# A low-rank gate product with its operands turned: activations stationary, 32 weight columns moving, sums in side banks and transposed back

## The reference, cut to what matters

```
h = rms_norm(x, norm_g)                  # (tokens, 2048)
proj = h @ w_in                          # c_lr: 16 of its columns
...
log_a = jax.nn.log_sigmoid((c_lr @ w_gate_lr + b_gate).astype(jnp.float32)) / C_GATE_TAU
o_c, new_S = gla_chunked(gq, gk, gv, log_a.reshape(bsz, L, C_HEADS, C_DK), gla_state)
```

## Time and profile before

| what | value |
|---|---|
| median of 3 runs | 2250.97 us (2250.37 to 2251.05) |
| profiled execution | 2249.99 us, its span 2248.2 us |
| TensorE busy (products, loads) | 2242.2 us, 2221.8 us |
| VectorE, ScalarE, GpSimd busy | 1378.3 us, 986.1 us, 77.6 us |
| share of the 16 DMA engines, mean rate | q1 42.7%, q0 5.3%; 162 GB/s |
| granted clock over the run | 1.00 |

### The profile page before, as it was taken

The page is one execution under the profiler, slowest core; times in us unless marked ns, Lnnn a source line. Parts: engine busy times, 40 slices in busy tenths (PEclk is TensorE's granted clock), DMA queues, the critical chain, the costliest instruction groups (busy, mean ns, idle before and its releaser), DMA issues.

```text
span 2248.2 us, 40404 instructions
## 1 busy us (share of the span) xinstructions
PE 2242.2 (100%) x16658; PEld 2221.8 (99%) x16658; DVE 1378.3 (61%) x2457; ACT 986.1 (44%) x1786; POOL 77.6 (3%) x122
## 2 busy tenths in 40 slices
PE   9999999999999999999999999999999999999999
PEld 9999999999999999999999999999999999999999
DVE  7777868765545555546657777777655545545443
ACT  6454356544333333333344543556443333333332
POOL 1100100000000000000011001000000000000000
DMA  8443754334444444445564447543344444444454
GB/s 301 147 160 125 242 197 148 114 131 150 149 149 150 149 149 150 149 150 196 191 227 134 160 134 243 196 141 113 132 150 150 150 150 150 151 150 150 151 198 149
DMA packets 100071, 364.12 MB, mean 162 GB/s; under 512 B 12288, under 2 KB 13056, under 8 KB 99056
## 3 DMA queue, kind: packets, MB, share of 16 engines
q1 hardware_dynamic: 89472, 318.91, 42.7%
q0 software_dynamic: 10128, 42.43, 5.3%
q10 hardware_dynamic: 288, 0.21, 0.0%
HBM read 341.65 MB, written 20.50 MB: 161 GB/s over the span
## 4 chain that ended last, share of the span: by engine, by line
PE 99%; DVE 1%; ACT 0%; issue 0%; ACTq 0%; DVEq 0%
PE main L1715 92%; PE side L1715 5%; PE side L1719 1%; PE side L1935 0%; ACT probs L1420 0%; PE side L1858 0%; DVE ta L536 0%; DVE w_lo L517 0%; DVE probs L947 0%; PE side L1942 0%; DVE probs L951 0%; PE side L1866 0%; DVE probs L912 0%; ACT w_hi L1229 0%; DVE probs L914 0%
## 5 line engine op out<-in xcount | busy, mean ns | idle before, releaser
L517 DVE TENSOR_TENSOR w_lo<-raw,w_hi 128x512 fp32r<-128x512 f32 x1184 | 785.3, 697 | 498.3 <-ACT w_hi L1229 492.9
L1715 PE MATMUL main<-xg_hi,w_hi 128*128 128x320 f32 x3488 | 1083.7, 311 | 2.2 <-DVE w_lo L517 2.2
L1715 PE MATMUL main<-xg_lo,w_hi 128*128 128x320 f32 x3488 | 1077.2, 309 | 0.0
L1715 PE MATMUL main<-xg_hi,w_lo 128*128 128x320 f32 x3456 | 1067.9, 309 | 0.0
L1229 ACT ACTIVATE w_hi<-raw 128x512 fp32r<-128x512 f32 x1184 | 709.6, 626 | 698.2 <-PE main L1715 667.8
L1715 PEld LDWEIGHTS main<-xg_hi,w_hi 128*128 128x128 f32 x3488 | 654.8, 188 | 6.0 <-DVE w_lo L517 2.7
L1715 PEld LDWEIGHTS main<-xg_lo,w_hi 128*128 128x128 f32 x3488 | 654.9, 188 | 0.0
L1715 PEld LDWEIGHTS main<-xg_hi,w_lo 128*128 128x128 f32 x3456 | 648.7, 188 | 0.0
L1715 PE MATMUL main<-branch_hi,w_hi 128*128 128x320 f32 x768 | 237.3, 309 | 0.0
L1715 PE MATMUL main<-branch_lo,w_hi 128*128 128x320 f32 x768 | 237.3, 309 | 0.0
L1715 PE MATMUL main<-branch_hi,w_lo 128*128 128x320 f32 x768 | 237.3, 309 | 0.0
(11 more groups left out here) (259 smaller groups left out, 1292.6 us busy)
## 6 DMA issues: line engine op xcount, KB each, us to landing
raw<-in_w_stream SPq DMA_DIRECT2D x595, 512.0 KB, 3.3
state<-in_state POOLq DMA_DIRECT2D x16, 512.0 KB, 4.7
out_state_s<-state POOLq DMA_DIRECT2D x16, 512.0 KB, 3.9
turned<-normed SPq DMA_DIRECT2D x40, 80.0 KB, 2.1
x_first<-in_x_pairs SPq DMA_DIRECT2D x7, 320.0 KB, 7.4
w_pool<-in_w_pool POOLq DMA_DIRECT2D x2, 1024.0 KB, 6.5
cache_k<-in_cache_k POOLq DMA_DIRECT2D x2, 1024.0 KB, 5.1
cache_v<-in_cache_v POOLq DMA_DIRECT2D x2, 1024.0 KB, 8.2
```

What stands on the lines that cost most here:

```text
L517: dve.tensor_tensor(w_lo[Q % RAWS][:, half], raw[Q % RAWS][:, half], w_hi[Q % HIS][:, half].bitcast(F32), ALU.subtract).then_inc(lo_ready, 1)
L1715: return pe.matmul(out, lhsT, rhs, start=start, stop=stop)
```

## The change

The operands of the rank products are turned. Each of the 16 k tiles of `xg_hi` and `xg_lo` is the stationary operand in three pieces of tokens (`TOKEN_TILES`: 128, 128 and 64), and the tile's 32 useful weight columns (16 high, 16 low) are moved. The sums, tokens on the partitions and 32 columns wide, gather in side banks 1, 2 and 3 in place of a bank of `main`. The four copies of the 16 columns are no longer made by the splits. Instead VectorE copies the finished sums out of PSUM four times side by side (`rank_tok`, which lies in the memory of `tc`), and `rank_turn`, after the block of beat 10, transposes the three pieces into side bank 0. VectorE scales that into `ta`. The gate step moves from beat 10 to 11, `log_decay_sum` from 12 to 13 and `decay_scan` from 13 to 14. The main group of the rank products is gone, so groups are numbered without it.

```diff
-    put(10, "gate", 0, (0, 1, 2, 3))
+    put(11, "gate", 0, (0, 1, 2, 3))
...
-            t = w_hi[Q % HIS][:, half].rearrange("p (k h c) -> p k h c", k=4, h=GH)
-            return t[:, :, :, at:at + RANK]
+            t = w_hi[Q % HIS][:, half].rearrange("p (k c) -> p k c", k=4)
+            return t[:, :, at:at + RANK]
...
-                    dve.tensor_tensor(ta[:, 0, :], group_psum(GROUPS * l + LR_GROUP)[:, 0, :], rstd[:, :],
-                                      ALU.mult).then_inc(main_free, 1)
-                    marks[("lr", l, 0)] = (main_free, GROUPS * l + LR_GROUP + 1)
-                if beat == 12:
+                    four = lambda t: t.unsqueeze(2).to_broadcast([t.shape[0], t.shape[1], 4, 2 * RANK])
+                    v(dve.tensor_copy(rank_tok[:, 0:2, :].rearrange("p i (q c) -> p i q c", q=4),
+                                      four(side[:, 1:3, 0:2 * RANK])))
+                    v(dve.tensor_copy(rank_tok[0:SMP, 2:3, :].rearrange("p i (q c) -> p i q c", q=4),
+                                      four(side[0:SMP, 3:4, 0:2 * RANK])))
+                    v.mark("rank_tok", l, 0)
+                if beat == LR_AT + 2:
+                    dve.wait_ge(rank_turned, l + 1)
+                    dve.tensor_tensor(ta[:, 0, :], rank_psum, rstd[:, :], ALU.mult).then_inc(rank_taken, 1)
+                    marks[("lr", l, 0)] = (rank_taken, l + 1)
+                if beat == 13:
                     log_decay_sum(l)
-                if beat == 13:
+                if beat == 14:
                     decay_scan(l)
...
-                out = main[:, 2 * (G % 2), 0:TOK]
                 for s in range(2):
                     pe.wait_ge(lo_ready, Q * 2 + (s + 1))
                     for kk in range(4):
-                        k, c = k0 + 4 * s + kk, 512 * s + P * kk
-                        both = w_hi[Q % HIS][:, c:c + P]
-                        mm(out, both, xg_hi[:, k, :], first and s == 0 and kk == 0, False)
-                        ins_ = mm(out, both, xg_lo[:, k, :], False, last and s == 1 and kk == 3)
+                        c = 512 * s + P * kk
+                        for x in (xg_hi, xg_lo):
+                            for i, (lo, hi) in enumerate(TOKEN_TILES):
+                                ins_ = mm(side[0:hi - lo, 1 + i, 0:2 * RANK], x[:, k0 + 4 * s + kk, lo:hi],
+                                          w_hi[Q % HIS][:, c:c + 2 * RANK], first and s == 0 and kk == 0 and x is xg_hi,
+                                          last and s == 1 and kk == 3 and x is xg_lo)
                     ins_.then_inc(half_used, 1)
+
+            def rank_turn(l):
+
+                if l == 0:
+                    pe.wait_ge(consts_in, 64)
+                wait_mark(pe, "rank_tok", l, 0)
+                wait_mark(pe, "rms_taken", l, 0)
+                for i, (lo, hi) in enumerate(TOKEN_TILES):
+                    last = turn(rank_psum[:, lo:hi], rank_tok[0:hi - lo, i, :])
+                last.then_inc(rank_turned, 1)
```

More of the change, by code:

```diff
@@ L57 @@
 BEATS = IN_BEATS + MIX_BEATS + OUT_BEATS
-GROUPS = 1 + N_IN + PAIRS * 6 + PAIRS
+GROUPS = N_IN + PAIRS * 6 + PAIRS
 BR_A, BR_B, BR_C = 0, 1, 2
@@ L68, in first_beat @@
     return 4 * g if g < LR_AT // 4 else LR_BEATS + 4 * g
-def group_no(g):
-    return g if g < LR_AT // 4 else g + 1
-LR_GROUP = LR_AT // 4
+TOKEN_TILES = ((0, P), (P, SEQ), (SEQ, TOK))
 C_COS, C_SIN, C_IDENT, C_BLOCK, C_KEEP, C_INVC, C_BSEL, C_END = 0, 320, 640, 768, 896, 1216, 1280, 1288
@@ L291, in trunk @@
         tb = place("tb", [P, 2, TOK])
+        rank_tok = place("rank_tok", [P, 3, P], at=top[0])
         tc = place("tc", [P, 2, TOK])
@@ L360, in trunk @@
         rms_psum = side[:, 0, 0:TOK]
+        rank_psum = side[:, 0, 0:TOK]
         raw_in = [sem(f"raw_in{i}") for i in range(RAWS)]
@@ L384, in trunk @@
         rms_done = sem("rms_done")
+        rank_turned = sem("rank_turned")
+        rank_taken = sem("rank_taken")
         x_hi_ready = sem("x_hi_ready")
@@ L474, in rank_columns @@
         def rank_columns(Q, half, at):
-            t = w_hi[Q % HIS][:, half].rearrange("p (k h c) -> p k h c", k=4, h=GH)
-            return t[:, :, :, at:at + RANK]
+            t = w_hi[Q % HIS][:, half].rearrange("p (k c) -> p k c", k=4)
+            return t[:, :, at:at + RANK]
         def rank_source(Q, half):
-            t = raw[Q % RAWS][:, half].rearrange("p (k c) -> p k c", k=4)[:, :, 0:RANK]
-            return t.unsqueeze(2).to_broadcast([P, 4, GH, RANK])
+            return raw[Q % RAWS][:, half].rearrange("p (k c) -> p k c", k=4)[:, :, 0:RANK]
         block = ctx.enter_context(nc.Block())
@@ L572, in take @@
             def take(l, g):
-                G = GROUPS * l + group_no(g)
+                G = GROUPS * l + g
                 end = last_half(l, first_beat(g) + 3)
@@ L1096, in mix_pair @@
                 Q0 = BEATS * l + IN_BEATS + 18 * j
-                G0 = GROUPS * l + 1 + N_IN + 6 * j
+                G0 = GROUPS * l + N_IN + 6 * j
                 for n in range(3):
@@ L1122, in out_pair @@
                 Q0 = BEATS * l + IN_BEATS + MIX_BEATS + 4 * j
-                G = GROUPS * l + 1 + N_IN + 6 * PAIRS + j
+                G = GROUPS * l + N_IN + 6 * PAIRS + j
                 for part in range(4):
@@ L1565, in store_y @@
             def store_y(l, j):
-                pool.wait_ge(main_free, GROUPS * l + 1 + N_IN + 6 * PAIRS + j + 1)
+                pool.wait_ge(main_free, GROUPS * l + N_IN + 6 * PAIRS + j + 1)
                 load((outs["y"] if l == DEPTH - 1 else ins["y_mid"])[j], (ta, tb)[j % 2][:, :, :], y_out[j % 2])
@@ L1719, in turn, with rank_products @@
                 return pe.transpose(out, src, ident[0:src.shape[0], 0:src.shape[0]])
-            def rank_products(Q, G, k0, first, last):
-                out = main[:, 2 * (G % 2), 0:TOK]
+            def rank_products(Q, k0, first, last):
                 for s in range(2):
@@ L1957, in _ @@
                     if LR_AT <= beat < LR_AT + LR_BEATS:
[L1958 to L1961, removed]
+                        part = beat - LR_AT
+                        rank_products(Q, 8 * part, part == 0, part == 1)
                     else:
                         g, part = divmod(beat if beat < LR_AT else beat - LR_BEATS, 4)
-                        G = GROUPS * l + group_no(g)
+                        G = GROUPS * l + g
                         if part == 0:
@@ L1975, in _ @@
                         mm(rms_psum, ones_r[:, :], rms_lo[:, :], False, True).then_inc(rms_done, 1)
+                    if beat == LR_AT + 2:
+                        rank_turn(l)
                     for name, k, banks in STEPS.get(beat, ()):
@@ L1980, in _ @@
                 Q = BEATS * l + IN_BEATS
-                G = GROUPS * l + 1 + N_IN
+                G = GROUPS * l + N_IN
                 for j in range(PAIRS):
```

## The result

The changed kernel takes 2273.2 us (median of 5 runs, 2270.37 to 2274.40), the kernel before on the same chip 2250.93 us (5 runs): a ratio of 1.0098, 95% interval [1.0087, 1.0109]. It is slower by 22.3 us. I had forecast slower by 9.9 us.

The account below looks back on a forecast made before the run. TensorE's issue, busy 2242.2 of 2248.2 us, was taken as the bound. Rank products +4.32 and turn +0.65 make 4.97 us per layer, twice 9.9, on 2250.97: 2260.9 us; own range 2258.5 to 2264, eight in ten 2256 to 2276.

Parts of the forecast that it names:

- Rank products: Per layer 32 sets of three load-paced products, 0.282 us each: 9.02 us in for 4.70 out, +4.32 us.
- Turn with its change-over: Three added transposes at the end of beat 10, including changing the array over and back: 0.65 us per layer.
- VectorE's copies: Two instructions copying the sums out during TensorE's 3.52 us beat 10: hidden; otherwise at most 1.6 us per layer.
- The margin behind the gate: VectorE's low parts after the gate come 0.4 us before TensorE wants them; costed at nothing, 0.5 us kept for the range.
- T: Start of the first block product after the gate; first low half forecast at T + 17.2, wanted at T + 17.6 us.
- the granted clock: Taken to stay at 1.00, the level of 2.4 GHz, in the rank stretch.
- a rival at 11%: Clock falls to 1.2 GHz in the rank stretch because the array moves little: +9 us per layer if throughout; 11%.
- the sign that I had named: A rank stretch of 17 us with a granted clock below 1.00 would show that the clock fell.
- the two sizes I gave: Times if the clock fell in the rank stretch: 2279 us for the whole stretch, 2270 us for half; 11%.
- The loads do pace: Against a rival where rank products go at their own columns' pace, 27 ns each: 2248.1 us; 4%.
- not half: Against a rival where a full load in the rank stretch counts 53 ns, not 106, a set about 160 ns: 2253.3 us; 7%.
- change the array over: Rival: each 64-token rank product pays about 0.21 us in and 0.21 out, a set some 0.55 us: 2278 us; 9%.

Follow-up runs that it names:

- three kernels: The changed kernel with 128 different columns moved per turned product, with the 32 useful ones moved four times, and with 96 moved: 2260.32, 2260.49 and 2260.62 us.
- the best turned form: The changed kernel with each turned product moving 128 columns of the weight buffer in place of 32, same loads: 2260.32 us, ratio 1.0042 to the kernel before.

## Why the prediction was wrong

**The other terms of the sum held.** Rank products: 0.282 us for a set, measured 0.282, and 9.06 us for the stretch at full clock (9.02). Turn with its change-over: 0.62 (0.65). VectorE's copies done while TensorE is in beat 10, no wait. The margin behind the gate held, at the place that I gave. VectorE in order of time, after:

```profile
75.32 1.12 DVE L1029 MEMSET lev_k<- 128x1280 f32 x1 [0.33 <-DVE cb L711]
76.36 1.22 DVE L515 TENSOR_TENSOR w_lo<-raw,w_hi 128x512 fp32r<-128x512 f32 x2
```

With the gate's successor at 59.82 the first low half is there at 76.36 + 0.61 = T + 17.15 (T + 17.2 in the working), and TensorE does not wait. With the clock at full the sum came out as written: 2260.3 to 2260.6 us in three kernels, for 2260.9.

**The step that failed is the granted clock, which the sum took at 1.00.** The prediction kept the fall apart, as a rival at 11%, and it is what came: stretches of 12.8 and 13.4 us with a granted clock of 0.50 in their later part (the sign that I had named was 17 us). The measured time is that of the sum, 2260.3 us at full clock, and 12.9 us of half clock. That it lies between the two sizes I gave, 2270 us for half of the stretch and 2279 for the whole, is in part luck: the first 3.9 to 4.6 us ran full and the rest at half, which is the smaller size, and the dense block behind paid 1.9 to 2.5 us per layer that I had not put in.

**What I weighed wrongly** was the evidence against it: "short side steps leave the stream at full pace". The thin ones among these side steps are short. The thinnest of before (TensorE in order of time) move 16 columns at a time:

```profile
84.33 0.96 PE L1715 MATMUL side<-lev_q,lev_k 128*32 128x16 f32 x80
85.22 0.41 PE L1715 MATMUL main<-xg_hi,w_hi 128*128 128x320 f32 x1
```

That is 0.9 us; the products with 32 moved columns of the earlier trace rows take 0.4 us. The longest side step, 5.2 us on end (from 186.01), moves 128 columns and more throughout. The stretch to judge was 9 us on end, ten times the thin ones, and I had said so myself: nowhere in before does it do so little for so long. The only row that showed TensorE at the low clock was its start, after idleness, and I read "never idle" as safe. The Trainium skill, "TensorE: Matmul & The Clock Gate", section on oscillation in real kernels, gives the rule in that form too, as one against gaps in which TensorE is idle. The trace goes beyond it: 4.53 of 4.53 us busy with products and with loads, and the clock fell.

**The other rivals.** The loads do pace (no stretch below 9 us). They count in full for float32r, not half. A product on 64 tokens in the rank stretch does not change the array over: such sets go at 0.282 us. But a transpose of 64 rows does cost 0.29 us more, as the turn's change-over was forecast. Two sums of rivals were off: a set with the gate's 0.42 us of changes is 0.282 + 0.42 = 0.70 us and not 0.55, so that rival stood for some 2288 us and not 2278; and a set of 0.160 us gives 2253.1 us and not 2253.3. Neither bears on the forecast.

The change therefore loses three times over: 96 loads of 94 ns on average where 32 products of 147 ns were, +4.4 us per layer; the turn, +0.6; and the half clock, +6.2 to 6.3. No order or width tried here beats the kernel before, since the first two stay: the best turned form is at 2260.3 us. As TensorE is 99% of the chain, what the turn spares ScalarE and VectorE (splits of 64 columns for 256) buys nothing.

## What to carry to other kernels

Before turning a product, count loads and not only moved columns: with short moving operands each load of 128 columns takes its 0.112 us at full clock whatever is moved, up to 128 columns. Ask of every stretch of some microseconds not whether TensorE is busy but how much it moves; where it is thin, moving idle columns along under the load cost no time and here saved 12.9 us (the turned form still loses 9.4). Once the clock falls, ordinary products behind the stretch pay as well, so compare the step of a kind of product that was not changed (0.147 and 0.267 us here) before and after.

## What the runs showed of the hardware that I had not expected

- The granted clock falls from 1.00 to 0.50 while TensorE issues without a gap: 3.9 to 4.7 us after the first thin product in the profiles where the whole stretch was thin (32 or 64 moved columns per load of 128 or 64). With 96 and 128 moved columns it stays at 1.00.
- The fall can come sooner, 2.5 us after the first thin product, and also when the thin work has been over for 0.8 us (layer 2 of the two kernels with half of the stretch thin).
- It stays at half for 6.8, 10.2 or 13.7 us, with dense work running, and for the same time in both layers of a kernel.
- A set with loads of 128, 128 and 64 float32r columns and 32 moved ones steps at 0.282 us at full clock and 0.533 at half: not quite double.
- Short thin and dense runs in turn can fall either way: the same kernel took 2262.0 us four times and 2277 twice.
- The load records of transposes are shorter than those of products, 137 to 141 ns against 192 for 128 columns, and yet both step at 0.11 us.
